# First output projection of a two-block sequence mixer: eight half-size products against Strassen's seven

## The reference

```
y_a = rmsnorm(y * silu(z_ssd), g_ssd)            # 512 x 2048
y_b = rmsnorm(u * sg * silu(z_mlp), g_mlp)       # 512 x 2048
out = rmsnorm(concat([y_a, y_b]) @ w_out, g_post)   # w_out: 4096 x 2048
x1  = x + gate * out
...
h = rms_norm(x1, norm_gain_2) * (1 + scale) + shift
proj = h @ w_in_2
```

## Time and profile before

| | us |
|---|---|
| median of 3 runs (2778.81, 2781.98, 2782.41) | 2781.98 |
| span of the profiled execution | 2778.7 |
| PE busy in it (13142 matmuls) | 2740.8 |
| DVE, ACT, POOL busy | 1471.3, 1061.1, 339.1 |
| mean granted TensorE clock | 0.998 of full |
| stage under change, first to last matmul | 1432.72 to 1784.11 |

### The profile page before, as it was taken

The page is one execution under the profiler, slowest core; times in us unless marked ns, Lnnn a source line. Parts: engine busy times, 40 slices in busy tenths (PEclk is TensorE's granted clock), DMA queues, the critical chain, the costliest instruction groups (busy, mean ns, idle before and its releaser), DMA issues. The chain is left out here.

```text
span 2778.7 us, 33018 instructions
## 1 busy us (share of the span) xinstructions
PE 2740.8 (99%) x13142; PEld 2231.2 (80%) x13142; DVE 1471.3 (53%) x1794; ACT 1061.1 (38%) x1420; POOL 339.1 (12%) x417
## 2 busy tenths in 40 slices
PE   6999999999999999999999999899999999999999
PEld 3688888888888888888888888788888888788787
DVE  2377767765565456766652332634445443533733
ACT  3332222334333333433332332535556553442611
POOL 2101000102233323331310000100000000000000
PEclk9999999999999999999999999999999999999999
DMA  9667766744545464555454433332222223223252
GB/s 399 254 234 260 274 233 251 278 159 154 179 146 169 156 185 151 160 169 175 150 190 180 134 113 99 119 102 83 84 83 89 78 83 103 87 91 99 102 179 91
DMA packets 162120, 439.34 MB, mean 158 GB/s; under 512 B 14768, under 2 KB 59824, under 8 KB 151728
## 3 DMA queue, kind: packets, MB, share of 16 engines
q1 hardware_dynamic: 122208, 303.08, 32.7%
q0 software_dynamic: 16944, 97.18, 9.9%
q10 hardware_dynamic: 22816, 36.97, 3.8%
HBM read 398.11 MB, written 39.06 MB: 157 GB/s over the span
## 5 line engine op out<-in xcount | busy, mean ns | idle before, releaser
L1650 DVE TENSOR_TENSOR WL<-RAW,WH 128x1024 fp32r<-128x1024 f32 (+1 forms) x424 | 519.0, 1232 | 744.9 <-ACT WH L1031 568.9
L437 PE MATMUL PB<-HH,WH 128*128 128x512 f32 x2048 | 818.6, 400 | 2.4 <-DVE WL L1650 2.4
L442 PE MATMUL PB<-HL,WH 128*128 128x512 f32 x2048 | 801.6, 391 | 0.0
L443 PE MATMUL PB<-HH,WL 128*128 128x512 f32 x2048 | 801.3, 391 | 0.0
L1031 ACT ACTIVATE WH<-RAW 128x1024 fp32r<-128x1024 f32 (+1 forms) x424 | 433.4, 1038 | 444.0 <-PE PB L549 252.6
L547 PE MATMUL PB<-WH,HH 128*128 128x512 f32 x1248 | 490.0, 393 | 1.6 <-ACT Kr L1031 0.8
L549 PE MATMUL PB<-WH,HL 128*128 128x512 f32 x1248 | 486.1, 390 | 0.0
L548 PE MATMUL PB<-WL,HH 128*128 128x512 f32 x1248 | 485.9, 389 | 0.0
L437 PEld LDWEIGHTS PB<-HH,WH 128*128 128x128 f32 x2048 | 385.0, 188 | 103.3 <-issue 22.6
L442 PEld LDWEIGHTS PB<-HL,WH 128*128 128x128 f32 x2048 | 385.6, 188 | 65.6 <-issue 3.1
L443 PEld LDWEIGHTS PB<-HH,WL 128*128 128x128 f32 x2048 | 385.0, 188 | 66.2
(11 more groups left out here) (326 smaller groups left out, 2534.4 us busy)
## 6 DMA issues: line engine op xcount, KB each, us to landing
RAW<-in_w_in_t SPq DMA_DIRECT2D x312, 512.0 KB, 3.6
AU<-in_w_ada POOLq DMA_DIRECT2D x64, 1024.0 KB, 5.5
RAW<-in_w_out_t SPq DMA_DIRECT2D x96, 512.0 KB, 3.6
bcb<-R SPq DMA_DIRECT2D x64, 256.0 KB, 6.1
S<-so ACTq DMA_DIRECT2D x24, 384.0 KB, 2.5
...
```

The lines of the kernel that those rows point to most:

```text
L437: h.matmul(banks[j], lh, m.HH[:, t, :], start=st, stop=False)
L442: h.matmul(banks[j], lh, m.HL[:, t, :], start=False, stop=False)
L443: ins = h.matmul(banks[j], ll, m.HH[:, t, :], start=False, stop=en)
L1650: return h.tensor_tensor(o, a, b, op)
```

## The change

The contraction of 4096 is cut into four quarters c, the output columns into two halves n. For each of these eight groups q = 2c + n the operands are 2 x 2 blocks: the activations A (256 tokens by 512 rows each) and the weights B (512 rows by 512 columns each). Seven products of blocks replace eight:

- phase 0: A11 B11; phase 1: S1 E; phase 2: A12 B21; phase 3: S2 F; phase 4: S4 B22; phase 5: S3 H; phase 6: A22 G
- S1 = A21 - A22, S2 = S1 - A11, S3 = A11 - A21, S4 = A12 + S2
- E = B11 + B12, F = E + B22, G = F + B21, H = B12 + B22

A phase is two units of weights (ab = 0, 1) by two token blocks (j = 0, 1) by two tiles by three matmuls of 128x512: 24 matmuls, all of j = 0 first. A unit is now used by 12 matmuls instead of 24, and there are 112 units instead of 64.

E and H are made by DMAs that POOL issues with an adding write into a buffer which a plain load of SP has filled (`sum_E`, `sum_H`); F and G are made by POOL with `tensor_tensor` of 128x1024 (`sum_F`, `sum_G`), and so are S1 to S4 (`sum_S`, for a quarter ahead of its use; those for quarters 1 to 3 run in groups 1, 3 and 5). The seven activation operands of a quarter ("forms") have high parts `FH` made by ACT and low parts `FL` made by DVE.

The results are collected in `O`: the product of phase 0 goes into four blocks of `O`, so ACT copies it out twice (`c1a`, `c1b`), and from the third group on POOL adds or subtracts it into three of them (`fold`, six operations of 128x512 a group, in groups 2 to 7). DVE takes phases 1 to 6 out of PSUM (`evacuate`, one operation for each j). Phases 5 and 6 accumulate into the banks of the phase before, so phase 6 can't start before DVE has taken out phase 5 for the same j.

Behind the stage, ten of sixteen multiplications by `gg` of whole token blocks go from DVE to POOL (`gain`, after the last `fold`), ahead of `first_factor(0)`. DVE calls `make_x1(0, ...)`, which waits for that factor, ahead of the last two `evacuate`.

```diff
-UNITS_IN, UNITS_OUT, UNITS_IN2, UNITS_OUT2 = 192, 64, 128, 32
+UNITS_IN, UNITS_OUT, UNITS_IN2, UNITS_OUT2 = 192, 112, 128, 32
...
+def forms_due(q, ph):
+    c = q // 2
+    if q == 0:
+        return {0: [(0, 3)], 1: [(0, 4)], 3: [(0, 5)], 4: [(0, 6)]}.get(ph, [])
+    if q % 2:
+        return [(c + 1, f) for f in {1: [0], 3: [1], 4: [2], 6: [3]}.get(ph, [])] if c < 3 else []
+    return [(c, f) for f in {0: [4], 1: [5], 2: [6]}.get(ph, [])]
...
+    def product(q, ph):
+        for j in range(2):
+            bank = PB[(X, Z, X, Y, Z, Y, Y)[ph][j]]
+            bank_ready(q, ph, j)
+            P.wait_ge(*at("fl", q // 2, ph))
+            for ab in range(2):
+                n = form_unit(q, ph, ab)
+                split_ready(n)
...
+                    ins = h.matmul(bank, xl, wh[:, tt, :], start=False, stop=p == 3, skip_group_check=True)
...
+            if q == 0:
+                step(bg2)
...
+    def first_product(q, j):
...
+        A.then(act(m.c1a[j], src, ACT.Copy, scale=r[:, j:j + 1]))
+        A.then(act(m.c1b[j], src, ACT.Copy, scale=r[:, 2 + j:3 + j]), "c1", q, j)
...
+    for q in range(GROUPS):
+        for ph in range(7):
+            u = form_unit(q, ph, 0)
+            if ph:
+                evacuate(q, ph - 1, 1)
+            elif q:
+                evacuate(q - 1, 6, 1)
+            if u + 2 < AT_IN2:
+                make(u + 2)
+                make(u + 3)
+            for c, f in forms_due(q, ph):
+                form_low(c, f)
+            if q == 0:
+                step(bg2, 2)
+                if ph == 5:
+                    drain(bg2)
...
+            if q == 7 and ph == 5:
+                gain_out(0)
+            if q == 7 and ph == 6:
+                make_x1(0, 0)
+                make_x1(0, 1)
+            evacuate(q, ph, 0)
...
+    def add_load(q, ph, row, col, ab, sem, *key):
+        h.dma_start(m.WP[pair_of(q, ph)][ab], I["w_out_t"][out_source(q, row, col, ab)], accum_op=ALU.add) \
+            .then_inc(*land(sem, *key))
...
+    def sum_F(q):
+        for ab in range(2):
+            x = m.WP[pair_of(q, 3)][ab]
+            G.wait_ge(*at("lo", form_unit(q, 1, ab)))
+            G.wait_ge(*at("B22", q, ab))
+            add(x, x, m.WP[pair_of(q, 4)][ab], ALU.add, "F", q, ab)
...
+    for q in range(GROUPS):
+        c, n = divmod(q, 2)
+        sum_H(q)
+        sum_F(q)
+        if c:
+            fold(q, "O22")
+        if n and c < 3:
+            sum_S(c + 1, 1)
+        if c:
+            fold(q, "O12")
+        if q == 0:
+            sum_S(0, 4)
+        if n and c < 3:
+            sum_S(c + 1, 2)
+            sum_S(c + 1, 3)
+        sum_G(q)
+        if c:
+            fold(q, "O21")
+        if n and c < 3:
+            sum_S(c + 1, 4)
+        if q < 7:
+            sum_E(q + 1)
...
+    for k in range(4):
+        gain(k, 0)
+        gain(k, 1)
+    gain(0, 2)
+    gain(1, 2)
     first_factor(0)
+    first_factor(1)
+    gain(2, 3)
+    gain(3, 3)
```

More of the change, by code:

```diff
@@ new lines, in tensor_program, with bank_ready @@
+    m.bank.update({(nm, j): b[j] for nm, b in (("X", X), ("Y", Y), ("Z", Z)) for j in range(2)})
+    def bank_ready(q, ph, j):
+        if q == 0 and ph in (0, 1, 3):
+            reuse((X, Z, X, Y)[ph][j])
+            return
+        if ph == 0:
+            P.wait_ge(*at("O11", q - 1, j))
+        elif ph == 1:
+            P.wait_ge(*at("O12", q - 1, j))
+        elif ph == 2:
+            P.wait_ge(*at("c1", q, j))
+        elif ph == 3:
+            P.wait_ge(*at("O21", q - 1, j))
+        elif ph == 4:
+            P.wait_ge(*at("O22a", q, j))
+        elif ph == 5:
+            P.wait_ge(*at("O12a", q, j))
+        else:
+            P.wait_ge(*at("O22", q, j))
@@ new lines, in tensor_program @@
+    for q in range(GROUPS):
+        for ph in range(7):
+            product(q, ph)
+            if q == 0 and ph == 5:
+                drain(bg2)
+                b, bank = take(hb, "gate sums")
+                P.wait_ge(*at("GA", 15))
+                column_sums(b, bank, m.GA, "gate sums")
+                drop(hb, b, ("rb sum",))
+    for j in range(2):
+        drop(main, X[j], ("O11", GROUPS - 1, j))
+    for j in range(2):
+        drop(main, Y[j], ("O21", GROUPS - 1, j))
+        drop(hb, Z[j], ("O12", GROUPS - 1, j))
@@ new lines, in take_first, with square_out @@
+    def take_first(q, j):
+        A.wait_ge(*at(*out_done(q, 2, j)))
+        for e in (("sg", 15), ("sgt", 15)) if q == 0 else (("gate sums",),):
+            A.wait_ge(*at(*e))
+        A.then(act(m.O[:, j, 1024 * q:1024 * q + 512], bank("X", j), ACT.Copy, scale=m.ra[:, j:j + 1]), "O11", q, j)
+    squared = []
+    def square_out(k, nb):
+        A.wait_ge(*at(*out_final(k, nb)))
+        if squared:
+            A.wait_ge(*at(*squared[-1]))
+        A.then(act(m.jk, m.O[:, k, 512 * nb:512 * nb + 512], ACT.Square, acc=m.ss2[:, k * 4 + nb:k * 4 + nb + 1]),
+               "O squared", nb, k)
+        squared.append(("O squared", nb, k))
@@ L1407, in scalar_program @@
     square_x1(2, 0)
-    square_out(3)
     square_x1(2, 1)
```

565 lines of the change are left out of this document (359 added, 206 removed).

## The result

| | before | after |
|---|---|---|
| median of the runs, us | 2781.78 (4 runs) | 2852.18 (2850.74 to 2854.99, 4 runs) |
| ratio, 95% interval | 1 | 1.0255 (1.0241 to 1.027) |
| span of the profiled execution | 2778.7 | 2848.8 |
| stage, first matmul to last | 351.4 | 408.7 |
| from there to the first matmul of the next projection | 13.1 | 28.2 |

The change makes the kernel 70 us slower (2.55%). Forecast were 28.5 us, and 60 at the upper end of the range. The two windows that answer to the earlier trace rows show where: the stage, and the gap behind it. Columns are window and length, then busy time and count of PE, PE's weight loads, DVE, ACT and POOL, then mean clock, DMA share, GB/s.

The account below looks back on a forecast made before the run. The prediction took PE's number of matmuls times its pace, plus its waits, as the bound. Matmuls removed -43.5, start +10, groups +49 and tail +13 gave +28.5 us, so 2810 us, range 2766 to 2842.

Parts of the forecast that it names:

- the waits in the stage: PE's waits in the stage, forecast at some 60 us, mostly for DVE's low parts `WL`.
- the tail: Behind the stage: the first factor waits for POOL's ten gains, the last scaling comes later; 13 us more (bounds 4 and 18).
- the adding DMAs are hidden: Loads for E and H: issued early enough to cost 0, up to 30 us if they take three times 7.2 us.
- Removing the matmuls: PE in the stage: 1536 matmuls become 1344, 192 x 0.227 = 43.5 us less if nothing else makes PE wait.
- The sum: Whole kernel: -43.5 + 10 + 49 + 13 = +28.5 us, giving a span of 2807.2 and a time of 2810.
- rival 4: PE's clock: if the gates' waits drop it to half, each costs some 4 us, 2818; no separate chance given.
- Strict turns: POOL's sums and DVE's two-SBUF-input operations alternate one by one; a pair with a 128x1024 sum costs 3.3 us.
- The groups: Groups 1 to 7 of the stage: POOL's sums delay DVE's low parts and so PE; 49 us (bounds 15 and 70).
- The start: Stage's beginning: `wsr` of gates 14 and 15 comes 6 and 4 us late behind low parts; 10 us (bounds 0.4 and 16).
- Rival 3: Stage: adding DMAs are late and PE waits for E at each group's start; 2875, chance 0.10.
- Rival 1: Stage: POOL's sums don't hinder PE, alternation costs only DVE's spare time; 2749, chance 0.12.
- Rival 2: Stage: DVE and POOL exclude each other, but only what the totals don't fit costs; 2771, chance 0.14.

Follow-up runs that it names:

- e1_tiny: Kernel after, with POOL's F, G, folds, gains and S1 to S4 of quarters 1 to 3 over 8 columns only (result incomplete): 2758.6 us.
- e10_pause: Kernel before, with six pauses put into PE's list in the stage, each waiting for three or six needless POOL sums: 2834.4 us.
- e3: Kernel after, with every POOL sum waiting until the one before it is finished: 2852.0 us.
- e9_all2: Kernel after, with F and G by adding DMAs, H's behind F's, one gate step ahead of the low parts, and the tail reordered: 2800.8 us.
- e2_hlate: Kernel after, with H's two adding DMAs behind F's two sums in POOL's list instead of ahead of them: 2838.5 us.
- e13_pool: Kernel after, with F ahead of H, H behind fold O22 and S1, each sum waiting for the last, one gate step earlier: 2827.5 us.
- e16_floor: Kernel after, F and G by adding DMAs, lists and tail reordered, POOL's folds, gains and later quarters' S1 to S4 over 8 columns (result incomplete): 2761.0 us.

## Why the prediction was right or wrong

Right were the sign and its mechanism in the large (POOL's sums hinder DVE, DVE hinders PE), nearly the waits in the stage (70 to 73 us; 59 were forecast), the tail (15 us more, forecast 13) and that the adding DMAs are hidden. Removing the matmuls was to give 43.5 us. It gave about 39: e1_tiny's stage without its 4.2 us of waits and 2.6 us lost at half clock is 312.7 us, against 351.4, since the new order runs at 0.231 us a matmul.

**The clock** is the term that was mis-sized. The sum had nothing for it, rival 4 gave it up to 8 us, and only for the two gates (some 4 us each, where a fall cost about 2), though the same text forecast some 60 us of waits. Row 3 of the earlier trace rows showed the clock at half behind before's single long pause. Eight of the stage's pauses were over 4 us; at the 2.7 us of e10_pause they come to 22, and three falls stood at shorter pauses. Half clock cost 23 us. Of the 42 us between 2810 and 2852 these 23 are the largest part; 14 are waits (72.8 for 59), 5 the pace of 0.231 us, 2 the tail, and the stage began 1.7 us earlier. Without the clock's 23 us the time would have been inside the range.

**"Strict turns"** The earlier trace rows was the second wrong step. In that stretch each of POOL's sums needed the one before, so DVE got in between them. The new code has independent sums in a row, and there low parts took 7.43, 9.08 and 17.77 us, not one pair's 3.3. It moved the waits from many small ones into few long ones, and so made them into clock falls; for the total of the waits it made no difference (e3).

The Trainium skill (SBUF — State Buffer, SBUF: two separate sides) says that whoever starts first, a DVE operation with two SBUF inputs or a GpSimd one, holds the shared pair for its whole instruction and the other blocks. The traces agree for one instruction (a sum's 2.4 us turned a low part of 1.2 into 3.4). In a run of independent operations the traces show GpSimd going on seven times in a row, 1573.31 to 1585.5 in e9_all2, while DVE waits.

**The groups.** The amounts by group came out near: waits of 8.4, 4.9, 11.3, 7.0, 15.7, 4.3 and 9.6 us in groups 1 to 7, for 6, 5, 11.5, 5, 11.5, 5 and 5, and behind group 0 the groups 3 and 5 were the longest (54.1 and 57.4 us, near 50 forecast). How they come about did not. In place of many small ones each group has one large wait. In groups 1, 2, 4 and 6 it is at phase 2 (4.5, 4.9, 7.0 and 4.3 us by the distances of starts): the low part of B21, loaded plainly, is shut out by F's sums and what follows them. In groups 3, 5 and 7 it is at phase 3, for F (5.4, 13.9 and 6.2 us): in 5 by the low part of 17.77 us, in 3 and 7 by the take-out that waits for a fold. Both sums and folds are so bunched because they stand behind H's adding DMA, at which POOL was idle 12 to 26 us. The prediction said that H is issued 20 us ahead of its use and took that for a good thing; it never asked what stands behind it in POOL's list, nor what DVE's take-outs wait for. How much is due to H is not settled: with F ahead of H (e2_hlate) these seven waits still came to 38 us of 46, with H behind the first folds too (e13_pool) all waits to 48 of 73.

**The start** came out at 11.1 us for a forecast 10, for another reason. The low parts ahead of `wsr` took their usual time. What was held up was `wsr` itself, one-input operations of 128x128, which took 7.94 us for four (0.86 before) beside POOL's two sums of F and S4 (rows of DVE, then of POOL):

```profile
1433.38 2.36 DVE L1766 TENSOR_TENSOR WL<-hold,WH 128x1024 fp32r<-128x1024 f32 x2
1435.66 1.22 DVE L1766 TENSOR_TENSOR FL<-E1s,FH 128x1024 fp32r<-128x1024 f32 x1
1437.18 7.94 DVE L1770 TENSOR_SCALAR wsr<-wsg,small 128x128 f32<-128x128 f32 x4 [0.30 <-DMA wsg<-in_w_s_t]
```

```profile
1437.17 4.97 POOL L2580 TENSOR_TENSOR hold<-hold,hold 128x1024 f32<-128x1024 f32 x2
1441.78 2.65 POOL L2580 TENSOR_TENSOR E<-F,E1s 128x1024 f32<-128x1024 f32 x1
```

**The tail's** size was right and its cause half right. After:

```profile
1820.20 17.32 POOL L2580 TENSOR_TENSOR O<-O,gg 128x512 f32<-128x512 f32 x10
1837.60 0.19 POOL L2457 TENSOR_SCALAR small<-small 128x1 f32<-128x1 f32 x1
```

```profile
1838.49 2.48 DVE L1774 SCALAR_TENSOR_TENSOR O<-O,small,XR 128x1024 f32<-128x1024 f32 x2 [5.19 <-POOL small L2454]
```

The factor did wait for the ten gains. But with gains over 8 columns only, 10.9 of the 15 us remain in e1_tiny and 9.4 in e16_floor.

**Rivals.** Rival 3 falls: PE's only wait for `WH` in the stage was 2.3 us, once, and e1 has none. The adding writes landed after 8.1 and 7.0 us, the plain loads beside them after 7.4 and 5.5:

```profile
RAW<-in_w_out_t SPq DMA_DIRECT2D x64, 512.0 KB, 5.5
hold<-in_w_out_t SPq DMA_DIRECT2D x48, 512.0 KB, 7.4
...
hold<-in_w_out_t POOLq DMA_DIRECT2D x20, 512.0 KB, 8.1
...
RAW<-in_w_out_t POOLq DMA_DIRECT2D x12, 512.0 KB, 7.0
```

The rule that a reducing transfer goes at half a copy's rate (the Trainium skill, Collectives: The Full Stack, The bandwidth ceiling) would have given some 7 us, an estimate from it and the earlier trace rows; the rows agree roughly with the time, though most of the increase is in the plain loads as well. Rival 1 describes a kernel that an experiment built: 2749 was forecast if sums hinder nothing, and e1_tiny measured 2758.6. Rival 2, only what doesn't fit costs, has 15 us of waits in its groups; they had 61.
